# A 32-token form for the first expert stage, one form of turned picks, and gate and up weights with eight rows in a row per partition

## What is computed

```python
g_logits = hf @ w_rg + b_rg                      # 4 groups; the best one is taken
e_logits = (hf @ w_re + b_re).reshape(..., 4, 4) # 4 experts in each group
e_val, e_idx = lax.top_k(e_in_group, 2)          # two experts of that group
combine = ...                                    # weight of each token for each of 16 experts
for e in range(16):
    he = jax.nn.silu(h @ w_gate[e]) * (h @ w_up[e])          # 1024 -> 512
    out = out + combine[..., e:e + 1] * (he @ w_down[e])     # 512 -> 1024
```

## Time and profile before

| | us |
|---|---|
| median of 3 runs | 2244.49 (2244.12 to 2249.08) |
| the profiled execution, whole | 2264.11 |
| its span in the profile | 2261.8 |
| TensorE busy (matmul) | 1965.1 (87%) |
| VectorE busy, ScalarE busy | 561.4, 380.1 |
| DMA, mean over the span | 274 GB/s |
| first expert stage: first product to last down | 399.8 to 671.3 |

### The profile page before, as it was taken

The page is one execution under the profiler, slowest core; times in us unless marked ns, Lnnn a source line. Parts: engine busy times, 40 slices in busy tenths (PEclk is TensorE's granted clock), DMA queues, the critical chain, the costliest instruction groups (busy, mean ns, idle before and its releaser), DMA issues.

```text
span 2261.8 us, 26769 instructions
## 1 busy us (share of the span) xinstructions
PE 1965.1 (87%) x9952; PEld 1057.7 (47%) x9953; DVE 561.4 (25%) x1068; ACT 380.1 (17%) x666; POOL 8.4 (0%) x25
## 2 busy tenths in 40 slices
PE   7979987999999998999968789889988878778786
PEld 5565644666654766654433244344434333233333
DVE  3443342122124102442222121121121222122213
ACT  1022201121222002332011110010111111111101
POOL 1000000000000000000000000000000000000000
PEclk9978988999999997999979899999999888999888
DMA  8851352899993535122339997879799999999970
GB/s 278 323 185 38 112 176 84 292 376 373 373 378 108 191 125 186 38 75 74 150 116 415 416 416 293 331 295 390 313 416 414 416 414 415 415 406 416 414 312 19
DMA packets 175449, 620.84 MB, mean 274 GB/s; under 512 B 12216, under 2 KB 21090, under 8 KB 142478
## 3 DMA queue, kind: packets, MB, share of 16 engines
q1 hardware_dynamic: 175038, 616.95, 70.3%
q10 hardware_dynamic: 208, 0.67, 0.1%
HBM read 616.55 MB, written 1.05 MB: 273 GB/s over the span
## 4 chain that ended last, share of the span: by engine, by line
PE 72%; DMA 16%; issue 4%; DVE 4%; ACT 3%; POOL 0%; ACTq 0%; DVEq 0%; SPq 0%; POOLq 0%
DMA ring<-exp_w 16%; PE pairs L1580 15%; PE pairs L1928 9%; PE pairs L1567 7%; PE pairs L1831 5%; PE pairs L1914 3%; PE pairs L2043 3%; PE pairs L2015 3%; PE pairs L1994 3%; PE pairs L2006 3%; PE pairs L1615 3%; PE pairs L1860 3%; PE pairs L1980 2%; PE pairs L1658 2%; PE pairs L1931 2%
## 5 line engine op out<-in xcount | busy, mean ns | idle before, releaser
L1928 PE MATMUL pairs<-ring,r_at 128*32 128x512 f32 (+2 forms) x1856 | 318.2, 682 | 101.2 <-issue 50.3
L1928 PEld LDWEIGHTS pairs<-ring,r_at 128*32 128x32 f32 (+2 forms) x1856 | 89.8, 129 | 302.5 <-issue 301.2
L1580 PE MATMUL pairs<-ring,x_T 128*128 128x512 f32 (+1 forms) x480 | 182.8, 537 | 2.5 <-ACT r_big L807 1.1
L1567 PE MATMUL pairs<-x_T,ring 128*128 128x256 f32 x656 | 153.6, 393 | 8.0 <-DVEq L936 6.6
L1994 PE MATMUL pairs<-ring,r_big 128*32 128x512 f32 (+1 forms) x896 | 122.8, 595 | 36.8 <-issue 36.8
L1567 PEld LDWEIGHTS pairs<-x_T,ring 128*128 128x128 f32 x656 | 126.4, 196 | 32.7 <-issue 8.0
L2043 PE MATMUL pairs<-r_at,r_big 128*128 128x512 f32 x264 | 135.0, 659 | 5.2 <-issue 3.9
L2015 PEld LDWEIGHTS pairs<-r_big,r_mix 128*128 128x128 f32 x1056 | 124.9, 194 | 18.0 <-issue 18.0
L1299 DVE TENSOR_SCALAR r_big<-r_u,rank 128x128 f32 x66 | 15.9, 284 | 456.2 <-PE pairs L1928 431.3
L1580 PEld LDWEIGHTS pairs<-ring,x_T 128*128 128x128 f32 x480 | 84.6, 193 | 94.3 <-issue 92.2
L2015 PE MATMUL pairs<-r_big,r_mix 128*128 128x128 f32 x1056 | 125.2, 278 | 2.4 <-DVE r_big L1299 2.4
(11 more groups left out here) (337 smaller groups left out, 1943.3 us busy)
## 6 DMA issues: line engine op xcount, KB each, us to landing
ring<-exp_w SPq DMA_DIRECT2D x192, 2048.0 KB, 20.8
ring<-w_in SPq DMA_DIRECT2D x23, 2048.0 KB, 8.9
ring<-w_gate SPq DMA_DIRECT2D x16, 2048.0 KB, 11.5
ring<-w_up SPq DMA_DIRECT2D x16, 2048.0 KB, 13.8
ring<-w_down SPq DMA_DIRECT2D x16, 2048.0 KB, 9.5
ring<-mod_w SPq DMA_DIRECT2D x12, 2048.0 KB, 13.5
ring<-w_out SPq DMA_DIRECT2D x4, 2048.0 KB, 7.9
ring<-w_branch SPq DMA_DIRECT2D x3, 2048.0 KB, 8.0
```

The lines of the kernel that those rows point to most:

```text
L1567: ins = mm(out[:, ct], w[:, k, c0 + P * ct:c0 + P * ct + P], xT[:, k], start=(k == 0), stop=(k == nk - 1 and bias is None))
L1580: ins = mm(out[:, t, 0:n], xT[:, k, P * t:P * t + P], w[:, k, c0:c0 + n], start=(k == 0), stop=(k == nk - 1 and bias is None))
L1928: ins = mm(out, stat(k), w_[:, k % 2, 512 * q:512 * q + 512], start=(k == 0), stop=False)
```

## The change

1. `sizes` of the first stage gets the four classes of the second (up to 32, 64, 128, above), with one more operation in `ranks`. All first-stage bodies go by `in_turn` (TensorE) or `smallest_first` (the others); `by_size` goes.
2. The new class has bodies of its own. Gate and up are one group of 32 matmuls, with 32 tokens as stationary operand and 256 columns each, in four column tiles of `ps[0]`: two for up, two for gate. The group waits for both loads, and raises `PD` by two at its end. Silu and the product with up are on 64 partitions by 256. The hidden values are turned by two transposes of 64 by 64. Down is 8 matmuls in four column tiles. Scatter is as for 64 tokens.
3. `picks` of the first stage reads its slots from a table, `slot_table[1]`, written once by VectorE (`slots_of_sizes`) and indexed by the expert's class. Turned picks are two transposes for every class.
4. Gate and up are read as `(p t) n -> p t n`: partition p gets rows 8p to 8p + 7, which are 16 KB in a row in DRAM and in SBUF. Down stays as it was. So that the features match, the transposes of the normed rows take every eighth column (`XN_by_rows`), the router weights are loaded the same way, and the gain comes by a load of its own (`gain1`).
5. ScalarE's body for an expert is cut into three branches (gate, next rows, outputs), with the copy of the turned picks after them.

```diff
-                src = w[bass.ds(e * (nk * P), nk * P), :].rearrange("(t p) n -> p t n", p=P)
+                rows = w[bass.ds(e * (nk * P), nk * P), :]
+                src = rows.rearrange("(t p) n -> p t n" if kind == 2 else "(p t) n -> p t n", p=P)
...
+                    if w == H4:
+                        ins = s.activation(SG[0:H2, 0:256], ps[0][H2:P, 0:256], ACT.Silu)
...
-                if n == NE2:
-                    link(v.tensor_scalar(some, cum[0:1, 0], float(P // 4), None, ALU.is_gt))
...
+                link(v.tensor_scalar(some, cum[0:1, 0], float(P // 4), None, ALU.is_gt))
+                link(v.scalar_tensor_tensor(out=some, in0=cum[0:1, 0], scalar=float(P // 2), in1=some,
+                                            op0=ALU.is_gt, op1=ALU.add))
...
-                slots = iota if b == 1 else slots_of[:, bass.ds(size_of(dve, e) * P, P)]
+                slots = slot_table[b][:, bass.ds((size_of(dve, e) if size is None else size) * P, P)]
...
-                        ins = nc.tensor.transpose(out[:, k, P * t:P * t + P], src[:, t, P * (k0 + k):P * (k0 + k) + P],
-                                                  ident)
+                        cols = src[:, t, k0 + k] if len(src.shape) == 4 else src[:, t, P * (k0 + k):P * (k0 + k) + P]
+                        ins = nc.tensor.transpose(out[:, k, P * t:P * t + P], cols, ident)
...
+                    if up and w != H4:
+                        pe.wait_ge(sem("pickT_ready1"), e + 1)
+                    if w == H4:
+                        both = (w_, slot1(j - 1, KD))
+                        parts = [(ps[0][H4 * q:H4 * q + H4, 0:256], lambda k: XG[:, k, 0:H4], both[q // 2], 256 * (q % 2), 256)
+                                 for q in range(4)]
...
+                    ins.then_inc(PD, 2 if w == H4 else 1)
+
+                in_turn(pe, size, body, (H4, H2, P, T) if up else (H2, P, T))
...
+                            if w == H4:
+
+                                at, to = H2 * (f % 2) + H4 * (f // 2), H2 * h + H4 * (f // 2)
+                                ins = mm(ps[2][to:to + H4, 0:512], HTF[:, at:at + H4], cols, start=(f % 2 == 0),
+                                         stop=(f % 2 == 1))
```

More of the change, by code:

```diff
@@ L776, in hidden_T2, with outputs_out @@
                 ins.then_inc(sem("hiddenT_ready2"), 1)
-            def outputs_and_picks(b, e, w, pd_down):
-                n = 512 if b == 1 and w == H2 else 1024
+            def outputs_out(b, e, w, pd_down):
+                n = 512 if b == 1 and w <= H2 else 1024
                 if b == 1 or w != T:
@@ L1196, in _, with slots_of_sizes @@
                     mod_scale(24, 24)
+            def slots_of_sizes(table):
+                for c, w in enumerate((H4, H2)):
+                    link(v.tensor_copy(table[:, P * c:P * c + P].rearrange("p (q s) -> p q s", s=w),
+                                       iota[:, 0:w].unsqueeze(1).broadcast_to([P, P // w, w])))
+                link(v.tensor_copy(table[:, 2 * P:4 * P].rearrange("p (q s) -> p q s", s=P),
+                                   iota.unsqueeze(1).broadcast_to([P, 2, P])))
             def routing_ahead(n, before_all):
@@ L1840, in body @@
                 def body(w):
-                    for c in range(4 * w // P):
-                        ins = nc.tensor.transpose(ps[1][:, P * c:P * c + P], src[:, P * c:P * c + P], ident)
+                    if w == H4:
+                        for c in range(2):
+                            ins = nc.tensor.transpose(ps[1][:, H2 * c:H2 * c + H2], src[0:H2, P * c:P * c + P],
+                                                      ident[0:H2, 0:H2])
+                    else:
+                        for c in range(4 * w // P):
+                            ins = nc.tensor.transpose(ps[1][:, P * c:P * c + P], src[:, P * c:P * c + P], ident)
                     ins.then_inc(sem("hidden_turned1"), 1)
-                by_size(pe, size, body)
+                in_turn(pe, size, body)
             def half_down(j, load_value, size):
                 pe.wait_ge(slot_loaded[j % RING], load_value)
-                w_ = ring[:, (j % RING) * SLOT:(j % RING + 1) * SLOT].rearrange("p (t n) -> p t n", t=4)
+                w_ = slot1(j, 4)
                 def body(w):
-                    for f in range(4):
+                    for f in (0, 2, 1, 3) if w == H4 else range(4):
                         beg, end = f == 0, f == 3
@@ L2045, in scatter2, with turn_picks @@
                 ins.then_inc(sem("scattered2"), 1)
-            def turn_picks1(buf, size):
-                def body(w):
-                    for t in range(NT):
-                        o = ps[1][:, P * t:P * t + P]
-                        if w == H2:
-                            for h in range(2):
-                                ins = mm(o[H2 * h:H2 * h + H2, :], pick[:, buf, t, 0:H2], ident, start=True, stop=True)
-                        else:
-                            ins = nc.tensor.transpose(o, pick[:, buf, t], ident)
-                    ins.then_inc(sem("pick_turned1"), 1)
-                by_size(pe, size, body)
-            def turn_picks2(buf):
+            def turn_picks(b, buf):
                 for t in range(NT):
                     ins = nc.tensor.transpose(ps[1][:, P * t:P * t + P], pick[:, buf, t], ident)
-                ins.then_inc(sem("pick_turned2"), 1)
+                ins.then_inc(sem(f"pick_turned{b}"), 1)
             def value_of(j, i, nk):
@@ L2084, in expert1 @@
                 half_down(j + 2, value_of(j + 2, i, 3), size)
-                turn_picks1(buf, size)
+                turn_picks(1, buf)
             def expert2(i, par, j, e, size):
```

102 lines of the change are left out of this document (54 added, 48 removed).

## The result

| | before | after |
|---|---|---|
| median, us (5 runs each) | 2244.49 (2241.30 to 2249.08) | 2266.08 (2259.06 to 2278.29) |
| ratio, 95% interval | 1 | 1.0092 (1.0063 to 1.0121) |
| profiled execution, whole and span | 2264.11, 2261.8 | 2278.29, 2274.6 |
| first stage, first product to last down | 399.8 to 671.3 (271.5) | 400.4 to 693.5 (293.1) |
| TensorE busy in the stage | 270.1 | 238.5 |

The forecast was 2214.5 (2205 to 2228), faster. The sign was wrong: TensorE works 31.6 us less in the stage, which lasts 21.6 us longer.

A forecast was written before the change was run, and what follows sets the result against it. TensorE was taken to bound the first stage, with transfers close behind (10% to spare at most). A 32 us gain there, less 1.0 and 1.0 us ahead of it, took 30 us off the median: 2214.5 us, range 2205 to 2228.

The forecast's parts named there:

- the last case: Other stalls, such as code loads behind the longer skips, take all of the gain; chance 0.05.
- TensorE's own sum: First stage: TensorE's products alone would end the last down at 622.1 us, said to be 9 us before the transfers.
- The new wait for silu: Small experts: silu and product (1.6 us) fit under the 1.92 us scatter; taken as 0, up to 0.6 us an expert.
- Transfers bind from about expert 8: First stage: 15.15 us of loads against 11.5 of products per small expert; last down at 639.2, gain 32 us.
- The spacings: First-stage weight loads land 5.05 us apart; 5.3 for gate and up would cost 4 us, 4.9 would gain 3.
- Rival 1: First stage: transfers do no better than now, loads 5.6 us apart, 12.6 us less gain, 2227 us; chance 0.17.
- rival 3: Gate and up loads: rows of 16 KB move worse; at 7.5 us a load 21 us slower, 2266 us; chance 0.05.
- Rival 2: Small experts: TensorE can't issue fast enough, gate and up stay at 6.9 us, 14 us gain, 2230 us; chance 0.10.
- Ahead of the stage: Chain to the first gather: one more operation in `ranks` and the class load in the first picks cost 1.0 us.
- The transposes with every eighth column: Ahead of the first stage: strided reads in 16 transposes cost 1.0 us, bounds 0 and 3.5.
- Nothing given back behind the stage: After the last down: the next weights land about 637 us, before their product at about 651; later parts move along unchanged.
- Clock: Experts 8 to 11: waits of 3.7 us each may lower TensorE's clock; taken as 0, with 5 us kept in the range.

The follow-up runs named there:

- e1: The changed kernel with TensorE's first-stage bodies for more than 64 tokens left out: 2201.9 us, ratio to before 0.9823.
- e9: The kernel of e1, run again unchanged: 2206.8 us, ratio to before 0.9826.
- e11: The changed kernel with TensorE's first stage written twice behind one branch (small forms alone, or all four), second run: 2216.8 us, ratio to before 0.9871.
- e10: The kernel of e1 with gate and up read in rows of 2 KB again: 2213.0 us, ratio to before 0.9864.
- e3: The kernel before with only the 16 KB rows of gate and up and the strided transposes added: 2246.3 us, ratio 1.0014.
- 9: Experiment on the second stage: 4 to 16 KB of never-taken matmuls put between the stages in e1's kernel; second stage 1068.7 to 1085.9 us.
- e12: The kernel before with TensorE's first-stage bodies for more than 64 tokens left out: 2243.0 us, ratio 0.9990.
- e2: The changed kernel with gate and up read in rows of 2 KB again: 2271.1 us, ratio to before 1.0116.
- e4: The changed kernel with all sixteen first-stage experts made to take the 64-token form: 2272.4 us, ratio to before 1.0115.
- e5: The kernel before with never-taken matmuls on TensorE, 32 behind up, 8 behind down, 4 behind the scatter: 2283.6 us, ratio 1.0186.
- e7: The changed kernel with TensorE's first stage written twice behind one branch (small forms alone, or all four), first run: 2224.9 us, ratio to before 0.9923.
- e14: The kernel of e1 with 32 never-taken matmuls (8 KB) between the stages: 2201.6 us, second stage 1068.7 us.
- e13: The kernel of e1 with 16 never-taken matmuls (4 KB) between the stages: 2217.5 us, second stage 1085.9 us.

## Why the prediction was wrong

**The step that failed is the sum itself.** It added executed matmuls and transfers, and no term for the program. Code loads stood in the last case alone, at 0.05, and only as "take all of the gain". They took 54 us in the first stage: after against e1, 293.1 - 238.7 = 54.4 us, which is 51.8 of waits more, 13.6 of TensorE's busy time more (238.5 against 224.9 for the same matmuls, at a mean granted clock of 0.95 against 0.99) and 11.2 less of waits for loads. The error behind it: the diff was costed by what experts execute, while the loads of code go by what is written. Skipped bodies had a price of nothing.

**The sign was in the rows.** The earlier trace rows have waits of 4.80 and 1.16 us that end in "issue", and the prediction used the first for the clock and never asked what TensorE waited for. The waits of before's second stage, had they been summed:

```profile
PE pairs L1928 <- issue: 50.3, 24, 9.2
PE pairs L1928 <- DMA ring<-exp_w: 49.9, 25, 4.3
PE pairs L1994 <- issue: 36.8, 28, 1.7
PE pairs L2064 <- issue: 15.6, 6, 2.7
PE pairs L1980 <- issue: 8.8, 4, 2.3
PE pairs L2043 <- issue: 3.9, 4, 1.2
```

115 us of "issue", in the stage that has the very form that the change brings to the first. How much of it is code loading no run separates: with a pad of 8 KB the waits ahead of up fell (62.7 us with 4 KB, 25.3 with 8), those ahead of down stayed (35.3 and 35.1). Still, this is the row to weigh against a plan to shorten an expert without shortening its code. And before's own stage gave a warning: 38 blocks came in 271.5 us, one in 7.1. With 189 matmuls an expert for 149, a quarter more code, the stage of 239 us needed one in 5.0, faster than before's stage had shown.

The Trainium skill has the rule ("Runtime: NRT & Kernel Launch", section "Instruction fetch mechanics"): the program streams in 16 KiB blocks, read ahead in sequence, and a taken branch to a target outside the window of two blocks stalls until it is fetched. The packets of 16.4 KB and the waits behind branches agree. The same section calls the fetching hidden by the pace of issue; for this stage the runs decide otherwise, with 54.2 us not hidden.

**Point by point.**
- A slip in the working: TensorE's own sum, 622.1, is 17 us short of 639.2, not 9. It changes nothing, since the transfers were on the path either way.
- Group 3.45 us, down 1.8, picks 0.37: right (3.66, 1.85, 0.37). In e1 a small expert that waits for nothing takes 11.6 us (460.71 to 472.35), forecast 11.5.
- The new wait for silu, 0: right. In e1 the turning follows the scatter with at most 0.3 us between.
- Transfers bind from about expert 8, the last down at 639.2, that is a stage of 239.4 us: wrong for after, where no load is ever late, and right once the code is out of the way, 238.7, 239.1 and 239.0 us in e1, e9 and e11. The first wait for a load there is ahead of expert 9 (e1, 524.54 us), and the five are 1.0 to 4.4 us long. That bears out the stage and not the time of 2214.5 us: the medians of e1 and e9, 2201.9 and 2206.8, hold a gain in the second stage too. The spacings: 4 us for the rows of 2 KB was too small (6.2 and 9.3, e10).
- Rival 1 (transfers no better) and rival 3 (16 KB rows worse) are refuted by e1 and e10. Rival 3's time, 2266, was that of after, by another cause. Rival 2 (issue rate) is refuted by 64 records in 3.66 us, 57 ns each. The Trainium skill ("TensorE: Matmul & The Clock Gate", section "Back-to-back issue gap") has about 62 ns as the floor for a MATMUL without hardware decoding, which would be 4.0 us; these rows are below it, and whether it applies on this chip no run shows.
- Ahead of the stage: the start of the whole stage moves by 8.5 us between two traces of one program (the gather begins at 385.37 us in e1 and at 393.90 in e9), so only the path from the transposes' start to the gather can be compared. It takes 17.38 us in before (374.23 to 391.61) and 18.61 in after (374.07 to 392.68): 1.2 us for 1.0. The transposes with every eighth column: 1.0 us taken, nothing measured; with them alone, in e3, the path is 17.45 us. In order of time, after, to be read beside the earlier trace rows:

```profile
374.07 3.68 PE L1611 MATMUL pairs<-ident,r_mix 128*128 128x128 f32 x16 [6.02 <-DVEq L945]
```

That is 3.68 for 3.67 us, both at a granted clock of 0.50. The Trainium skill ("SBUF — State Buffer", section "Door 1: The DMA port swizzle") has a penalty for each access that goes to a new line of 16 bytes; it didn't show here, and at the higher clock no run tried it.
- Nothing given back behind the stage: right for the second mixer, which takes 500.1 us in before and 498.9 in after. The second stage did change, 1090.4 to 1082.2 us, as it does with the loop's place in the program (9), which the sum didn't know. This is also why e1 and e9 gain more (43 and 39 us) than their first stages (33 and 32): their second stage is 15 to 18 us shorter than that of e3 and e12.
- The profile's excess of before over its median, 0.9%, was not named. Against e3's trace 6 us of it lie ahead of the first stage (399.8 against 393.9), 9 in the second mixer (500.1 against 491.3) and 4 in the second stage (1090.4 against 1086.7).
- Clock, 0 to 5 us: 13.6, since the waits were other and longer ones.

## What to carry to other kernels

A written-out stage with a branch for each size pays for every form it holds, taken or not. So count a form twice, by what it executes and by what it adds to the program, and set the blocks of an expert against the time that it is to last: here one block of 16.4 KB, 64 fp32 matmuls, came in 6.1 us beside the weights. Sum the waits named "issue" before shortening anything; where rare forms are needed, put them into a second copy of the stage behind one branch.

## What the runs showed of the hardware

- TensorE's program comes at one packet of 16.4 KB in 6.1 to 6.2 us in four kernels in which it binds (after, e2, e4, e5), with 322 to 341 GB/s of traffic in all, and in 5.1 us or less with 136 GB/s. A packet itself takes about 1 us in both. The program is 0.8 MB of some 100 in the stage, and the stage waits for it all the same.
- An fp32 matmul is 256 bytes of program: 40, 82 and 84 of them an expert more or fewer are 10, 21 and 21 packets (after against before, e1 against after, e12 against before).
- A jump over some 0.8 MB of program costs one wait of 5.0 to 5.7 us, and that code isn't loaded (181 and 182 packets in e11 and e7, 179 in e1); bodies of a few KB that are skipped are loaded (200 packets whether or not an expert takes the small form, e4).
- The same loop takes 1068.7 to 1085.9 us by where it lies in the program (e14, e13), one trace each.
